# Order of VectorE's weight splits and evacuations at four stage borders of a two-block transformer kernel

## What is computed

```python
def first_block(x, c, ...):
    mod = silu(c) @ w_ada + b_ada                      # six vectors: shift, scale, gate (twice)
    h = modulate(rms_norm(x, g_mix), sh_m, sc_m)
    qa, ka, va, qb, kb, vb, gate_logits = split(h @ w_in)
    ya = moba_attention(qa, ka, va) @ w_br_moba        # "the branches"
    yb = stick_breaking_attention(qb, kb, vb) @ w_br_sb
    g_a, g_b = split(sigmoid(gate_logits))
    x = x + gt_m * ((g_a * ya + g_b * yb) @ w_out)     # "the projection"
    h2 = modulate(rms_norm(x, g_ffn), sh_f, sc_f)
    u_val, u_gate = split(causal_depthwise_conv(h2 @ w_up))
    x = x + gt_f * ((gelu(u_gate) * u_val) @ w_down)   # "the feed-forward", 11 steps
    return rms_norm(x, g_final)
# second block: even layer  x + gt * (even_mix(pre(x)) @ e_w_out), the same for the context,
#               odd layer   x + gt * (odd_mix(pre(x), pre(ctx)) @ o_w_out), final norm
```

## Time and profile before

| | us |
|---|---|
| median of 3 runs | 806.34 (805.28 to 806.70) |
| the profiled execution | 805.59 |
| its span | 803.8 |
| PE busy | 753.2 (94%) |
| DVE busy | 647.7 (81%) |
| ACT busy | 388.3 (48%) |
| POOL busy | 42.9 (5%) |
| splits (L862), 93 | 212.6, 2.29 each |
| casts (L371), 93 | 176.9, 1.91 each |

### The profile page before, as it was taken

How to read it: one execution, slowest core, us unless ns; L and a number is a source line. 1 busy time by engine, 2 the same in 40 slices (tenths; PEclk the granted TensorE clock), 3 DMA queues, 4 the chain that set the end, 5 groups by cost and what they waited for, 6 DMA issues and landing times.

```text
span 803.8 us, 13124 instructions
## 1 busy us (share of the span) xinstructions
PE 753.2 (94%) x5479; PEld 698.4 (87%) x5480; DVE 647.7 (81%) x1001; ACT 388.3 (48%) x521; POOL 42.9 (5%) x31
## 2 busy tenths in 40 slices
PE   0399999999899999999998999999999999999996
PEld 0399999999798999999998998888777899899995
DVE  3987777994796799999889659999989956886752
ACT  2354645557447555454546532321464334455742
POOL 0000000000000222223311000000000000000000
PEclk9899999999999999999999999999999999999999
DMA  9999998765453666776645142213106632663101
GB/s 346 415 346 366 356 355 312 257 232 201 171 210 117 208 252 214 265 259 259 252 168 209 54 177 85 82 77 104 53 0 232 216 146 88 231 233 137 53 1 53
DMA packets 26086, 156.58 MB, mean 195 GB/s; under 512 B 2691, under 2 KB 7084, under 8 KB 7852
## 3 DMA queue, kind: packets, MB, share of 16 engines
q1 hardware_dynamic: 21392, 148.91, 50.0%
q10 hardware_dynamic: 4636, 6.85, 2.6%
HBM read 154.68 MB, written 1.06 MB: 194 GB/s over the span
## 4 chain that ended last, share of the span: by engine, by line
PE 72%; DVE 15%; ACT 5%; issue 4%; ACTq 1%; DMA 1%; POOL 1%; DVEq 0%
PE psum L1332 60%; DVE w_lo L829 5%; DVE w_lo L862 3%; ACT w_hi L371 2%; PE psum L1367 1%; PE psum L1624 1%; PE psum L1798 1%; DMA raw<-in_w 1%; PE psum L1774 1%; PE psum L1786 1%; PE psum L1610 1%; PE psum L1474 1%; DVE xs L1186 1%; POOL arena L336 1%; DVE arena L1023 1%
## 5 line engine op out<-in xcount | busy, mean ns | idle before, releaser
L1332 PE MATMUL psum<-h_hi,w_hi 128*128 128x256 f32 (+1 forms) x1312 | 398.5, 304 | 15.8 <-DVE h_lo L902 10.0
L1332 PE MATMUL psum<-h_lo,w_hi 128*128 128x256 f32 (+1 forms) x1312 | 393.1, 300 | 0.0
L1332 PE MATMUL psum<-h_hi,w_lo 128*128 128x256 f32 (+1 forms) x1312 | 393.1, 300 | 0.0
L1332 PEld LDWEIGHTS psum<-h_hi,w_hi 128*128 128x128 f32 x1312 | 252.0, 192 | 28.0 <-issue 14.5
L862 DVE TENSOR_TENSOR w_lo<-raw,w_hi 128x2048 fp32r<-128x2048 f32 x93 | 212.6, 2288 | 61.0 <-ACT w_hi L371 60.2
L1332 PEld LDWEIGHTS psum<-h_lo,w_hi 128*128 128x128 f32 x1312 | 252.2, 192 | 7.7 <-issue 0.2
L1332 PEld LDWEIGHTS psum<-h_hi,w_lo 128*128 128x128 f32 x1312 | 252.1, 192 | 7.6
L371 ACT CAST w_hi<-raw 128x2048 fp32r<-128x2048 f32 x93 | 176.9, 1906 | 19.6 <-DMA raw<-in_w 15.3
L829 DVE SCALAR_TENSOR_TENSOR w_lo<-raw,cond 128x1024 fp32r<-128x1024 f32 x88 | 119.4, 1394 | 8.4 <-PE psum L1332 7.5
L829 DVE SCALAR_TENSOR_TENSOR w_lo<-raw,arena 128x1024 fp32r<-128x1024 f32 x48 | 56.8, 1221 | 1.1 <-DMA raw<-in_w 0.4
L1332 PE MATMUL psum<-g_hi,w_hi 128*128 128x256 f32 x160 | 45.8, 286 | 1.5 <-DVE w_lo L862 1.4
(11 more groups left out here) (214 smaller groups left out, 779.0 us busy)
## 6 DMA issues: line engine op xcount, KB each, us to landing
raw<-in_w SPq DMA_DIRECT2D x141, 1024.0 KB, 4.9
xs<-in_xs ACTq DMA_DIRECT2D x2, 1024.0 KB, 12.3
consts<-diff ACTq DMA_DIRECT2D x8, 128.0 KB, 6.5
cond<-in_cond ACTq DMA_DIRECT2D x1, 1024.0 KB, 6.8
out<-xs SPq DMA_DIRECT2D x4, 256.0 KB, 2.4
arena<-in_cond ACTq DMA_DIRECT2D x1, 512.0 KB, 7.0
consts<-in_c ACTq DMA_DIRECT2D x1, 512.0 KB, 3.6
arena<-in_c ACTq DMA_DIRECT2D x1, 448.0 KB, 3.2
```

The lines of the kernel that those rows point to most:

```text
L1332: last = mm(out, w[a], x[b], start=start and n == 0, stop=stop and n == 2, skip_group_check=skip)
```

## The change

VectorE's list: at the branches the evacuation of a chunk comes ahead of the next split; splits 23, 24 and 25 move behind L990, L992 and L984. In the projection's last round only the modulation product before chunk 29 stands ahead of the last evacuation; split 29 follows it. At the end of the feed-forward split 62 moves behind the eight evacuations of x. On the approach to the odd layer split 77 moves behind the first two evacuations of chunk 75. ScalarE's list: cast 23 moves ahead of the loads of the DFT constants, a table load and the eight squares of the context; in steps 0 and 9 of the feed-forward the cast of the next value part (casts 32 and 58) moves from behind g_hi to right behind gelu. No instruction is added or removed.

```diff
 # ScalarE
+            split(LIN_BR + 3)
             act.wait_ge(sem("pv_stick"), 4)
             act.dma_start(consts[:, 0:1024], c2_d[:, 0:1024]).then_inc(sem("c2_loaded"), 16)
...
-            for i in range(4):
-                if i:
-                    split(LIN_BR + i + 2)
-                if i == 0:
-
-                    load_ln_exp()
-                    act.wait_ge(sem("ctx_loaded"), 16)
-                    for k in range(KT):
-                        square("even_ctx", k)
-                if i % 2:
-                    n = i // 2
-                    act.wait_ge(sem("mixed"), n + 1)
-                    nc.scalar.copy(h_hi[:, 4 * n:4 * n + 4, 0:T],
...
+            load_ln_exp()
+            act.wait_ge(sem("ctx_loaded"), 16)
+            for k in range(KT):
+                square("even_ctx", k)
+            for n in range(2):
+                act.wait_ge(sem("mixed"), n + 1)
+                nc.scalar.copy(h_hi[:, 4 * n:4 * n + 4, 0:T],
...
+                if n == 0:
+                    split(LIN_OUT)
+                    split(LIN_OUT + 1)
...
+            CAST_FIRST = (0, FF_STEPS - 2)
+
             def value_part(c):
 
                 j = ffn_up(c)
-                split(j + 2)
+                if c - 1 not in CAST_FIRST:
+                    split(j + 2)
...
                 nc.scalar.activation(cg, cg, ACT.Gelu_apprx_tanh).then_inc(sem("gelu_done"), 1)
+                if c in CAST_FIRST:
+                    split(ffn_up(c + 1) + 2)
                 act.wait_ge(sem("ffn_mult"), c + 1)
...
 # VectorE, branches
             for i in range(4):
-                split(LIN_BR + i + 2)
...
                     nc.vector.tensor_tensor(m, src, g, ALU.mult).then_inc(sem("br_evac"), 1)
+                    split(LIN_BR + i + (2 if n == 0 else 3))
...
                     nc.vector.tensor_tensor(m, m, mix2, ALU.add).then_inc(sem("mixed"), 1)
+                    if n == 0:
+                        split(LIN_BR + 3)
                     dve.wait_ge(sem("mixed_hi"), n + 1)
...
+                    if n == 0:
+                        split(LIN_OUT)
 # VectorE, projection
+                elif i == 3:
+                    for m in mods_before(LIN_FFN + 1):
+                        mod_static(m, LIN_FFN + 1)
                 else:
                     split(LIN_OUT + i + 2)
...
+            split(LIN_FFN + 1, done=len(mods_before(LIN_FFN + 1)))
             norm("ffn", 2)
 # VectorE, end of the feed-forward
             split(ffn_down(FF_STEPS - 2) + 2)
-            split(ffn_down(FF_STEPS - 1) + 2)
...
+            split(ffn_down(FF_STEPS - 1) + 2)
             norm("even_x", 5, rstd_of=rstd2)
 # VectorE, approach to the odd layer
-                else:
+                elif i < 2:
                     split(LIN_EOUT + i + 2)
...
                 eout_evac(3, t, 0)
+            split(LIN_OIN + 1)
             norm("odd_x", 7)
```

More of the change, by code:

```diff
@@ L533, in _ @@
             act.dma_start(fw, fw_d).then_inc(sem("c2_loaded"), 16)
[L535 to L548 removed]
+            load_ln_exp()
[5 more added lines that the diff above has]
+                nc.scalar.copy(h_hi[:, 4 * n:4 * n + 4, 0:T],
+                               mix[:, 1024 * n:1024 * (n + 1)].rearrange("p (k n) -> p k n", n=T)).then_inc(sem("mixed_hi"), 1)
+                if n == 0:
+                    split(LIN_OUT)
+                    split(LIN_OUT + 1)
             for i in range(4):
```

1 line of the change is left out of this document (removed).

## The result

| | before | after |
|---|---|---|
| median of 4 runs, us | 805.86 (805.28 to 806.70) | 796.05 (795.57 to 796.50) |
| ratio to before | | 0.9878 (0.9866 to 0.989) |
| the profiled execution | 805.59 | 795.57 |
| its span | 803.8 | 793.8 |

The account below looks back on a forecast made before the run. PE, busy 94% of the span, bounds the kernel; only its waits can be gained. Terms -4.4 - 1.1 + 0.05 - 2.2 - 1.55 = -9.2 us took the median 806.34 to 797.1 us, range 795.2 to 799.6.

Parts of the forecast that it names:

- branches: At the branches, PE reaches the projection's second half at 216.5 instead of 220.80 us: -4.3, -4.4 with one restart less.
- projection, last evacuations: Projection's last round: evacuations come 2.2 us sooner, so PE's 0.99 us wait for squares goes with its restart: -1.1 us.
- cast first in step 0: Feed-forward start: PE saves 0.8 us at split 32 but waits for split 35 instead: +0.05 us net.
- step 9, cast first: Feed-forward step 9: PE's 0.8 us wait for split 58 goes, but the last down chunk starts only 0.25 us earlier.
- end of the feed-forward, with step 9: Evacuations no longer wait behind split 62, so PE's square sums start at 439.1: -2.2 us, 0.25 of step 9 included.
- odd approach: Approach to the odd layer: PE's 1.3 us wait for the evacuation behind split 77 goes, with restart: -1.55 us.
- The covers: Moved splits finish before the norm's rstd comes: cover 1.2 us for split 29, 2.1 for split 77; split 62 covered too.
- B: Rival: new waits at thin margins or in the feed-forward take part of the gain, about 798.6 us; chance 0.13.
- C: Rival: POOL and VectorE don't block each other where the split comes first and L339 second, 794.8 us; chance 0.09.
- E: Rival: the edits don't reach PE, for instance cast 23 waits for its load; 802.6 us; chance 0.04.
- D: Rival: PE's clock drops to half in denser stretches, 5.1 us each; from three on slower, 812.4 us; chance 0.02.
- the step from the profiled execution to the median: Whole kernel: the median of the runs lies 0.75 us above the profiled execution, 797.1 against 796.4 us.

Follow-up runs that it names:

- both undone: The changed kernel with casts 32 and 58 (steps 0 and 9) back behind g_hi: 795.96 us, ratio 0.9878.

## Why the prediction was right, and where it was off

| step | predicted, us | shown, us | by |
|---|---|---|---|
| branches | -4.4 | -4.40 | norm ffn -5.66, less the projection |
| projection, last evacuations | -1.1 | -1.26 | projection undone |
| cast first in step 0 | +0.05 | +0.08 at chunk 35, +0.17 later | marks; only step 0's cast undone |
| step 9, cast first | -0.25 | -0.23 | marks of both undone against step 0's undone |
| end of the feed-forward, with step 9 | -2.2 | -2.02 from chunk 35 to the sums | marks; undone: 1.88 and 0.23 for step 9 |
| odd approach | -1.55 | -1.56 | odd approach undone |
| sum | -9.2 | -9.16 | marks at the end |

**Right.** The reading of the waits, the sum, and each of its terms within 0.2 us. The four gains add up, as PE has no other wait between them: the shift at each mark is carried to the next. The prices held because each was worked out along the lists from rows, with the restart of PE in it. One small sign was missed: 0.3 to 0.5 us of wait were said to be left before the sums at the end of the feed-forward, and 0.25 are. The covers held too: norm ffn's first instruction started 1.11 us after split 29, the norm before the even layer 0.47 after split 62, the one before the odd layer 2.02 after split 77, and no wait of PE for chunk 29, 62 or 77 appeared. VectorE's timelines at the three places:

```profile
235.86 2.28 DVE L865 TENSOR_TENSOR w_lo<-raw,w_hi 128x2048 fp32r<-128x2048 f32 x1
239.25 1.28 DVE L899 SCALAR_TENSOR_TENSOR att<-xs,coef,rstd 128x256 f32<-128x256 f32 x3 [1.11 <-ACT rstd L398]
...
436.19 2.28 DVE L865 TENSOR_TENSOR w_lo<-raw,w_hi 128x2048 fp32r<-128x2048 f32 x1
438.94 1.28 DVE L899 SCALAR_TENSOR_TENSOR att<-xs,coef,arena 128x256 f32<-128x256 f32 x3 [0.47 <-ACT arena L619]
...
635.06 2.28 DVE L865 TENSOR_TENSOR w_lo<-raw,w_hi 128x2048 fp32r<-128x2048 f32 x1
639.36 1.28 DVE L899 SCALAR_TENSOR_TENSOR att<-xs,coef,rstd 128x256 f32<-128x256 f32 x3 [2.02 <-ACT rstd L398]
```

**The collision in step 0.** The prediction let L339 end 1.15 us behind the split, from rows of L336 beside another split; it ended 1.16 us behind it. The 0.8 us that PE saves at chunk 32 are lost again at chunk 35, and TensorE's new wait there was named (0.8 said, 0.75 shown). The edit looks good at the place where it is made and is worth nothing three chunks on.

**The rivals.** B (new waits): two are new, 0.75 us for split 35 and 0.91 us for POOL's last low part, and both are in the working of the sum. C: out, by the run in which VectorE waits for L339; that the kernel with those low parts on VectorE comes near C's 794.8 us (794.12) is no support for C, since it moves more than C spoke of. E: out; the branches gave all of their 4.4 us. D had the clock fall in the denser stretches and cost time. The clock did matter, but the other way round: it fell at a stop, and the change takes the stop away. D's ground was also misread in two places, without harm to the sum. The longest wait of PE isn't the 9.8 us but one of 11.4 us ahead of it, and there is one of 10.0 us before that:

```profile
PE psum L1367 <- ACT att L388: 13.0, 3, 11.4
...
PE psum L1394 <- DMA arena<-in_c: 10.0, 1, 10.0
```

And the clock at half didn't begin after the 9.8 us stop: it began at 33.3, inside it (28.3 to 38.1).

**The term that was mis-sized** is the last one, the step from the profiled execution to the median ("the median of the runs is 0.75 us above it"), carried over unchanged. Two things are wrong with it. First, the 0.75 isn't a constant of the kernel. Before's median of three, 806.34, lies in the upper of its two groups, its profile in the lower; after, whose stop is 0.25 us, has no gap in its four runs (795.57 to 796.50; mean clock 0.990 or 0.991). The medians of before in the five comparisons lie 0.1 to 1.0 us above 805.36, the lower group's own, by how many executions fall in the upper group, and no row of its profile shows that. Second, the profile that I summed against was itself a late starter: P0 came at 192.45, where the fourteen profiles lie between 191.58 and 192.45 with a median of 191.96. (PE's wait for `h_lo` at the start, 9.8 us in before and 8.9 in after, doesn't tell a late start: it is 9.9 in the kernel with step 0's cast undone, whose P0 is 191.94.) Its own time less the sum is 805.59 - 9.16 = 796.43; less those 0.5 us of start it is 795.9, for a measured median of 796.05. So the sum was right and the base was not: predicted 797.1, with the profiled execution as the base 796.4. And of the 9.8 us between the medians 9.2 are the edits; the median of before beside after, 805.86, lies 0.5 us above its lower group's, which is about the rest.

**What stays open:** what decides, from one execution to the next, whether the clock falls at the 2.15 us stop; why the gap between before's groups (1.06 us) is less than the 1.54 us of the profiles; and whether the moment at which the clock rises at the start is what makes a start late, and so the 0.5 us that before with the filler has over before.

## What to carry to other kernels

Where PE waits for an evacuation that waits behind a preparation for a later chunk in the same engine's list, put the evacuation first and check the cover of the preparation from the rows: four such places gave 9.2 us, each within 0.2 us of its working. Follow an edit to the next place that has no room: moving a cast earlier gained 0.8 us at one chunk and lost it three chunks on, since it drove VectorE's split into POOL's subtraction. And look at the runs as well as the profile: where the times of one kernel fall into two groups and PE has a stop of about 2 us, removing the stop may be worth more than the stop itself (here 1.5 us of clock on top of the 1.9 of the order, for a stop of 2.16 us), and filling it may bring the clock's part alone.

## What the hardware showed that was not expected

- **The clock after a short stop.** With a stop of 2.15 or 2.16 us, and full speed ahead of it, the granted clock was 0.50 for 3.40 us from 0.15 us ahead of the restart in one profile and 0.74 us behind it in another, and 1.00 throughout in a third with the same stop. The half clock costs 1.54 us. Eight zero matmuls in the stop (1.90 us) brought 1.45 us on one kernel (799.42 to 797.97) and 1.5 us in the median on another (806.28 to 804.81), about 1.0 of it by leaving no run in the upper group. The stops of 0.75 and 0.91 us in after are followed by a full clock. The Trainium skill ("TensorE: Matmul & The Clock Gate", section "Part 1: The HAM clock gate") has two states of the clock gate, half and full, and has the point at which the clock rises at a kernel's start differ from run to run. The trace agrees with the two states (0.50 and 1.00 in the stretches above) and with the second: behind the same start the clock rose between 41.13 and 43.68 us in the fourteen profiles. That the fall at a stop differs from one execution to the next is what the runs here show.
- **One matmul stream doesn't mean one time.** The forty runs of before fall into two groups 1.1 us apart, and only the lower group has been profiled. None of the 21 runs of the upper group whose mean clock is on record has the 0.992 that nine of the lower group's 14 have.
- **POOL's subtraction is slower than VectorE's even alone:** 1.29 us against 0.69 for 128 x 512, and 2.88 to 3.02 us when a split starts ahead of it. The split that starts ahead of it keeps its 2.29 us: POOL, coming second, bears the whole wait.
- **The other way round VectorE waits, which the working didn't see.** In steps 1 to 7 of the feed-forward, in before and in after, POOL's L339 starts first and an instruction of a modulation product (1.22 us by itself) second. That instruction then takes 2.31 us and ends 1.09 us behind L339. The one ahead of it, which runs beside the late L336 (277.83 to 280.44), starts at 279.20, takes 2.32 us and ends 1.08 us behind L336. In before's step 1:

```profile
281.16 1.51 POOL L339 TENSOR_TENSOR g_lo<-arena,g_hi 128x512 fp32r<-128x512 f32 x1 [0.73 <-ACT g_hi L593]
...
281.45 2.31 DVE L829 SCALAR_TENSOR_TENSOR w_lo<-raw,cond 128x1024 fp32r<-128x1024 f32 x1
...
284.95 1.22 DVE L829 SCALAR_TENSOR_TENSOR w_lo<-raw,cond 128x1024 fp32r<-128x1024 f32 x1
```

  Fourteen of the 136 instructions of modulation products (13 of 2.3 us, one of 2.19) read so, two in each of the seven steps, 2.2 us of the 16.86 us that VectorE is busy in a step. So part of what fills VectorE there is POOL. PE doesn't stand still for it in these steps, and no run took POOL's work away from them.
